# Gated delta rule: the substitution of the 32x32 blocks on GpSimd, with other places for merges, weight loads and splits

## What is computed

```python
proj = h @ w_in                                   # q, k, v, z, beta, a
qkv = silu(causal_depthwise_conv(qkv, conv_w))    # four taps
q, k = l2norm(q) * dh**-0.5, l2norm(k)            # each head used by two value heads
gc = cumsum(g, axis=-1)                           # g from a; per chunk
decay = exp(where(lower, gc[:, None] - gc[None, :], -inf))
a_mat = where(strict, (k * beta) @ k.T * decay, 0)
t_mat = triangular_solve(a_mat + eye, eye)        # inverse of a unit lower triangle
u, w = t_mat @ (v * beta), t_mat @ (k * beta * exp(gc))
qk = where(lower, q @ k.T * decay, 0)
# over the chunks, in order:
v_new = u - w @ state
o = (q * exp(gc)) @ state + qk @ v_new
state = state * exp(g_last) + (k * exp(g_last - gc)).T @ v_new
```

## Time and profile before

| | |
|---|---|
| median of 3 runs | 2576.68 us (2567.54, 2576.68, 2577.74) |
| the profiled execution's own time | 2569.33 us |
| its span, first to last instruction | 2567.5 us |
| granted TensorE clock, mean | 0.924 |
| busy: TensorE / its weight loads | 2159.8 us (84%) / 1669.2 us (65%) |
| busy: VectorE, ScalarE, GpSimd | 1160.5 us (45%), 852.3 us (33%), 500.0 us (19%) |
| L702 to L704, the slices, 784 each | 349.3, 316.8 and 315.8 us |

### The profile page before, as it was taken

The page is one execution under the profiler, slowest core; times in us unless marked ns, Lnnn a source line. Parts: engine busy times, 40 slices in busy tenths (PEclk is TensorE's granted clock), DMA queues, the critical chain, the costliest instruction groups (busy, mean ns, idle before and its releaser), DMA issues. The chain is left out here.

```text
span 2567.5 us, 29131 instructions
## 1 busy us (share of the span) xinstructions
PE 2159.8 (84%) x11176; PEld 1669.2 (65%) x11176; DVE 1160.5 (45%) x2121; ACT 852.3 (33%) x1288; POOL 500.0 (19%) x280
## 2 busy tenths in 40 slices
PE   3588989998898989657798299989989887999978
PEld 2466767776676767545586186667766655788767
DVE  5657566665657474415512432323324231532243
ACT  2354343434343444113301313332333452420031
POOL 0220202010111111004425421111111100532140
PEclk7799999999999999768999699999999898999989
DMA  6122323222222231225312121021120204211222
GB/s 264 48 82 59 103 58 95 53 92 56 88 59 89 57 98 59 52 101 188 110 48 76 52 61 50 25 99 34 50 74 26 74 25 164 90 58 50 74 82 82
DMA packets 126521, 199.21 MB, mean 78 GB/s; under 512 B 56324, under 2 KB 87812, under 8 KB 125232
## 3 DMA queue, kind: packets, MB, share of 16 engines
q1 hardware_dynamic: 126384, 197.34, 24.0%
HBM read 155.17 MB, written 42.11 MB: 77 GB/s over the span
## 5 line engine op out<-in xcount | busy, mean ns | idle before, releaser
L702 PE MATMUL p_job<-h_hi,w_hi 128*128 128x512 f32 x784 | 349.3, 446 | 87.3 <-DVE w_lo L847 83.0
L703 PE MATMUL p_job<-h_lo,w_hi 128*128 128x512 f32 x784 | 316.8, 404 | 0.0
L704 PE MATMUL p_job<-h_hi,w_lo 128*128 128x512 f32 x784 | 315.8, 403 | 0.0
L1688 PE MATMUL m_job<-h_hi,m_hi 128*128 128x512 f32 x592 | 262.0, 443 | 36.7 <-POOL m_lo L1524 36.7
L702 PEld LDWEIGHTS p_job<-h_hi,w_hi 128*128 128x128 f32 x784 | 153.9, 196 | 135.9 <-DVE w_lo L847 94.5
L1690 PE MATMUL m_job<-h_hi,m_lo 128*128 128x512 f32 x592 | 238.7, 403 | 0.0
L1689 PE MATMUL m_job<-h_lo,m_hi 128*128 128x512 f32 x592 | 238.0, 402 | 0.0
L1524 POOL TENSOR_TENSOR m_lo<-m_raw,m_hi 128x1024 fp32r<-128x1024 f32 x37 | 89.9, 2429 | 467.0 <-DVE m_hi L1796 467.0
L703 PEld LDWEIGHTS p_job<-h_lo,w_hi 128*128 128x128 f32 x784 | 154.2, 197 | 34.8 <-issue 7.7
L704 PEld LDWEIGHTS p_job<-h_hi,w_lo 128*128 128x128 f32 x784 | 153.7, 196 | 34.3
L1688 PEld LDWEIGHTS m_job<-h_hi,m_hi 128*128 128x128 f32 x592 | 115.3, 195 | 83.0 <-POOL m_lo L1524 37.4
(11 more groups left out here) (341 smaller groups left out, 4513.7 us busy)
## 6 DMA issues: line engine op xcount, KB each, us to landing
w_raw<-in_w SPq DMA_DIRECT2D x49, 512.0 KB, 3.9
m_raw<-in_w SPq DMA_DIRECT2D x37, 512.0 KB, 3.6
rows<-grows SPq DMA_DIRECT2D x32, 512.0 KB, 6.7
ada<-in_ada_w SPq DMA_DIRECT2D x8, 1536.0 KB, 12.6
e_raw<-in_w SPq DMA_DIRECT2D x24, 512.0 KB, 3.5
z_scr<-pre SPq DMA_DIRECT2D x16, 512.0 KB
o_scr<-oT SPq DMA_DIRECT2D x64, 128.0 KB, 1.8
ob<-o_scr SPq DMA_DIRECT2D x16, 512.0 KB, 4.5
```

Of the source, the lines that this page charges most:

```text
L702: nc.tensor.matmul(p_job[h][:], hi, h_hi[:, k, cut], start=(k == 0), stop=False)
L703: nc.tensor.matmul(p_job[h][:], hi, h_lo[:, k, cut], start=False, stop=False)
L704: last = nc.tensor.matmul(p_job[h][:], lo, h_hi[:, k, cut], start=False, stop=(k == KD - 1))
L1688: nc.tensor.matmul(p_job[h][:], hi, h_hi[:, k, cut], start=(k == 0), stop=False)
```

## The change

The lane steps move from VectorE to GpSimd, in the same form: 62 instructions and the turned copy in each of eight groups. Four numbers in `plan` move: `AHEAD` from 12 to 10, five slices and not four behind each lane step (so `lanes_out` stands behind slice 50 and not 44), and the merges behind slice 78 and not 72. The split stands ahead of a job's slice 1 and not of slice 6. The load ahead of slice 2 is of the job after the next, not of the next. In the lines below L972, L975 and L979 of before are L535, L538 and L542 of the change, and what stands between L523 and L960 is 19 lines further down (L845 is L864, L894 is L913, L910 is L929).

```diff
--- before.py
+++ after.py
@@ -210,7 +210,7 @@
 
 JOBS = 6
 SLOTS = NT + 2
-AHEAD = 12
+AHEAD = 10
 
 
 def plan(i):
@@ -244,10 +244,10 @@
         nonlocal sent, behind
         for _ in range(min(n, len(slices) - sent)):
             s = slices[sent]
-            if s[2:] == (0, 2):
+            if s[2:] == (0, 1):
+                out.append(("split", s[1]))
+            elif s[2:] == (0, 2):
                 out.append(("weights", s[1]))
-            elif s[2:] == (0, 6):
-                out.append(("split", s[1]))
             out.append(s)
             sent += 1
             behind = [(n - 1, x) for n, x in behind]
@@ -282,11 +282,11 @@
     send(AHEAD - sent)
     for q in range(LANE_STEPS):
         out.append(("lane", q))
-        send(4)
+        send(5)
         if ahead and q == 2:
             out.append(("bcast", i))
     out.extend([("lanes_out",), ("diag_in",)])
-    send(72 - sent)
+    send(78 - sent)
     if ahead:
         out.append(("decay", i, 0))
     for q in range(4):
@@ -447,8 +447,8 @@
                 for i in range(N_IT):
                     g = i - 1
                     for s in plans[i]:
-                        if s[0] == "weights" and 2 < job(i, s[1]) + 1 < N_JOBS:
-                            load(job(i, s[1]) + 1)
+                        if s[0] == "weights" and 2 < job(i, s[1]) + 2 < N_JOBS:
+                            load(job(i, s[1]) + 2)
                         elif s[0] == "bcast":
 
                             if i == 0:
@@ -522,7 +522,26 @@
                 for i in range(N_IT):
                     g = i - 1
                     for s in plans[i]:
-                        if s[0] == "decay":
+                        if s[0] == "lane":
+                            q = s[1]
+                            if q == 0:
+                                pool.wait_ge(al_in, 16 * (g + 1))
+                                pool.wait_ge(eye_in, 16 * (g + 1))
+                            for j in range(4 * q, min(4 * q + 4, BLK - 1)):
+                                m, r, w = N_LANE * g + 2 * j, j + 1, BLK - 1 - j
+                                step = lane_tmp[0:LANES, 0:r * w].rearrange("p (c i) -> p c i", i=w)
+                                if m >= 1:
+                                    pool.wait_ge(lane_done, m)
+                                nc.gpsimd.tensor_tensor(step, bc(UL[0:LANES, 0:r, j], 2, w),
+                                                        bc(AL[0:LANES, j, r:], 1, r), ALU.mult).then_inc(lane_done, 1)
+                                pool.wait_ge(lane_done, m + 1)
+                                nc.gpsimd.tensor_tensor(UL[0:LANES, 0:r, r:], UL[0:LANES, 0:r, r:], step,
+                                                        ALU.subtract).then_inc(lane_done, 1)
+                            if q == LANE_STEPS - 1:
+                                pool.wait_ge(lane_done, N_LANE * (g + 1))
+                                nc.gpsimd.tensor_copy(TL[0:LANES], UL[0:LANES].rearrange("p c t -> p t c")
+                                                      ).then_inc(turned, 1)
+                        elif s[0] == "decay":
                             b = s[2]
                             pool.wait_ge(diff_done, 4 * i + b + 1)
                             x = gams(i, b).rearrange("p a b c -> p (a b) c")
@@ -959,25 +978,6 @@
                                 kd[:, 2 * b:2 * b + 2],
                                 bc(p_mone[:, 0:256].rearrange("p (t c) -> p t c", t=2), 2, 2),
                                 bc(edl[:, 2 * b:2 * b + 2, :], 3, P), ALU.mult).then_inc(kd_done, 1)
-                        elif s[0] == "lane":
-                            q = s[1]
-                            if q == 0:
-                                dve.wait_ge(al_in, 16 * (g + 1))
-                                dve.wait_ge(eye_in, 16 * (g + 1))
-                            for j in range(4 * q, min(4 * q + 4, BLK - 1)):
-                                m, r, w = N_LANE * g + 2 * j, j + 1, BLK - 1 - j
-                                step = lane_tmp[0:LANES, 0:r * w].rearrange("p (c i) -> p c i", i=w)
-                                if m >= 1:
-                                    dve.wait_ge(lane_done, m)
-                                nc.vector.tensor_tensor(step, bc(UL[0:LANES, 0:r, j], 2, w),
-                                                        bc(AL[0:LANES, j, r:], 1, r), ALU.mult).then_inc(lane_done, 1)
-                                dve.wait_ge(lane_done, m + 1)
-                                nc.vector.tensor_tensor(UL[0:LANES, 0:r, r:], UL[0:LANES, 0:r, r:], step,
-                                                        ALU.subtract).then_inc(lane_done, 1)
-                            if q == LANE_STEPS - 1:
-                                dve.wait_ge(lane_done, N_LANE * (g + 1))
-                                nc.vector.tensor_copy(TL[0:LANES], UL[0:LANES].rearrange("p c t -> p t c")
-                                                      ).then_inc(turned, 1)
                         elif s[0] == "merge":
                             q = s[1]
                             dve.wait_ge(merge_ready, 4 * g + q + 1)
```

## The result

The changed kernel takes 2664.95 us (median of 4 runs, 2662.78 to 2668.28), the kernel before in the same runs 2577.21 us: a ratio of 1.0349, 95% interval 1.032 to 1.0378, so 3.5% or 87.7 us slower. The forecast was 2670.

What follows compares the result with a forecast made beforehand. The second stage was taken as bound by TensorE, stalled by late weight splits. Seven groups at 6.5 + 4.7 - 0.5 + 1.5 = 12.2 us (85), plus 15 for the last, on 2569.3 gave 2670 us; range 2615 to 2735.

Steps and rivals of the forecast that it cites:

- term 6: TensorE's clock: two slow stretches go, one idle stretch of 13 us comes; +1.5 us a group (0 to 4).
- step 1: Earlier loads and splits remove TensorE's weight stalls: slice 78 is reached 6.8 us earlier than the merge before.
- 2, chain with nothing beside it (last group): Lanes and turned copy on GpSimd, without VectorE's interference: 42.2 us (bounds 29 and 44).
- step 3: VectorE's taps, splits and norm multiplies hold up GpSimd's lanes through SBUF: 12.6 us a group (bounds 0 and 20).
- step 4: Last job's weight load, behind the substitution's seven loads on SyncE, delays the second merge: +4.7 us a group (0 to 7).
- Step 5: Recurrence: three chunks lose their slices; -0.5 us a group (0 to -1.2).
- Step 7: Last group: the turned copy ends later on GpSimd, all of it on the path; +15.4 us (3 to 25).
- the 40 to 44 that were named as a sign: Sign of being right: last group's chain, AL's landing to end of turned copy, takes 40 to 44 us.
- Rival A: Lane instructions slip between VectorE's without blocking, but the last load stays late: 2571 us; chance 0.08.
- Rival B: Short instructions cost GpSimd less and hardly block, a chain of 34 us: faster, 2525 us; chance 0.12.
- Rival C: Short rows or blocking cost GpSimd's lanes 15 us more in each of eight groups: 2790 us; chance 0.06.
- Slice 72 at 475.3: Without stalls and slow matmuls, TensorE would come to the first merge at 475.3 us instead of 486.21.

Runs made afterwards that it cites:

- short_taps: The change with VectorE's three taps of each convolution cut from 1024 columns to 8, leaving work out: 2576.34 us, ratio 1.0008.
- load_before_stores: The change with the weights load at slice 0 instead of 2, so the last job's load precedes the substitution's two stores: 2653.26 us, ratio 1.0319.
- norm_sums_later: early_weights_only with the two key norm sums and their multiplies placed 4 to 8 slices later, and one added VectorE wait: 2586.85 us, ratio 1.0045.
- norm_behind_copies: early_weights_only with the second query norm behind its half job's copy, key norms after it, and an added VectorE wait: 2582.69 us, ratio 1.0037.
- norm_copies_70: norm_behind_copies with the merges behind 70 slices instead of 72 and an added SyncE wait between stores of z: 2587.99 us, ratio 1.0063.
- norm_later_merge_68: norm_sums_later with the merges behind 68 slices instead of 72 and an added SyncE wait between stores of z: 2604.97 us, ratio 1.0121.
- hi_on_scalar: early_weights_only with the rounding of weights to their high part on ScalarE from the fourth job on: 2558.16 us, ratio 0.9947.
- early_weights_only: The kernel before with only the earlier weight loads and splits; lanes on VectorE, merges at slice 72: 2551.86 us, ratio 0.9928.

## Why the prediction was right

The forecast of slower and its size, 2670 against 2665, came out mostly by its own mechanism; the clock of term 6 had another cause than the one named, and the closeness of the two numbers is in part luck. The rows for a group are those of i = 3:

| step | predicted, us | measured, us |
|---|---|---|
| 1, slice 78 done, after the first slice | 58.1 | 56.8 |
| 2, chain with nothing beside it (last group) | 42.2 | 39.7 |
| 3, added by VectorE | 12.6 | 13.3 |
| chain in the group | 54.8 | 53.0 |
| merge later | +6.5 | +4.3 |
| 4, second merge after the first | +4.7 | +4.2 |
| 5, recurrence | -0.5 | 0 |
| 6, clock, second merge to read | +1.5 | +2.7 |
| a group | 12.2 | 11.2 (11.4 in the mean of six, 12.1 up to the read of i = 1) |
| 7, last group | +15.4 | +12.0, and 7.8 in its chunks |
| later stages | 0 | -3.2 |

*Steps 1 to 3.* From the end of slice 78 to the first merge TensorE is idle for 12.40 us, where 10 to 15 were named. The merge is 2.2 us less late than forecast: AL landed 7.6 us after the first slice and not 8.1, and the chain was 1.8 shorter. With nothing beside them the 31-element instructions took 0.24 to 0.26 us and those of 252 to 256 elements 0.63 to 0.72 rather than 0.73, the multiplies less than the subtractions; the turned copy took 1.90 and not 1.5. The last group's chain, 39.7 us, is just below the 40 to 44 that were named as a sign. short_taps bears out what step 3 gives to the nine taps, 7.9 us: without them the chain was 6.8 to 8.6 us shorter in groups i = 2 to 7, 7.6 in the mean. The edits to group i = 0, put at nothing, moved the first slice of i = 1 from 160.68 to 162.17 us.

The lane instruction beside a tap took 1.5 us, and three taps in a row 4.88 where they take 3.92 alone. GpSimd got through about three lane instructions in that time; three taps and three of these at 0.65 to 0.68 us each would be 5.9 us end to end. The Trainium skill's rule (SBUF — State Buffer, "SBUF: two separate sides"), by which the lock holds for a whole instruction and the loser blocks fully, would have made step 3 20 us, by the prediction's estimate; 13.3 was measured. The block itself the trace confirms, and where GpSimd's instruction is long it is nearly whole. In the same group VectorE's cast, 0.69 us alone, took 4.77 beside the product for the queries:

```profile
447.80 4.60 POOL L567 TENSOR_TENSOR qd<-qd,qv 128x2048 f32<-128x2048 f32 x1 [5.41 <-ACT qd L676]
```

```profile
448.18 4.77 DVE L864 CAST w_hi<-w_raw 128x1024 fp32r<-128x1024 f32 x1
```

No wait of TensorE came of it, but the subtract behind it now fell beside the first lane instruction, which took 1.22 us in place of 0.24. The prediction did not look at this pair, which the earlier split brings together.

*Step 4* was right in mechanism and within half a microsecond. load_before_stores shows it as the load's place in the queue, and that getting rid of it lengthens step 3.

*Step 5 failed*: the recurrence took 35.5 us both times. Before, the steps from read to read already went 5.32, 4.93, 5.31, 4.94, 5.32, 4.93, with slices in all but the last; so the 5.32 and 4.93 of the earlier trace rows were odd and even chunks, and not chunks with slices and without. In the change three chunks lost their slices. Two steps fell from 5.3 to 5.04, but two rose from 4.93 to 5.20, the last among them, which held no slices either way.

*Step 6* was undersized by 1.2 us, and its cause was misplaced. It named the idle time ahead of the first merge. In the full groups of the fourteen traces the stretch from the second merge to the first read took 11.8 to 12.4 us wherever TensorE waited at most 1.5 us ahead of the second merge, and 13.6 to 15.1 us wherever it waited 3.2 us or more. The idle time ahead of the first merge makes no such difference: the low figures hold after 15.8 to 18.5 us of it in load_before_stores and after 18.28 in the change's own group i = 1; the high ones hold in norm_sums_later, norm_behind_copies, norm_copies_70 and norm_later_merge_68, which have none. So the 2.7 us go with the wait of step 4, and moving the load takes both away. The idle time ahead of the first merge shows in the work up to the second, at a clock of 0.59 in load_before_stores and 0.69 in the change. In the change this cost nothing of its own, since TensorE waits there for the copy in any case.

*Step 7* has two parts in the measurement. The merge was 12.0 us later relative to the group's first slice, where 15.4 stood; the prediction costed nothing for the recurrence behind it, which took 49.2 us in place of 41.4. Other kernels have 49.2 us after 18.6 and 19.4 us of idle and 42.6 after 33.5, so this 7.8 us may be scatter of the clock in the last group and not the change's doing; one trace of each kernel can't settle it.

*The sum.* What the prediction priced adds up to 100.8 us; the same parts measured, up to the last group's merge, are 12.1 + 68.5 + 12.0 = 92.6. In the profiled pair the 7.8 us of the last chunks make up most of the difference, and the later stages give 3.2 back; their code is the same, and over the fourteen traces they took 1434 to 1446 us. Without the 7.8 us this execution would have taken about 2659. The forecast also started from 2569.3 us, one execution; from the median before, 2577.2, the same sum would have said 2678. Between the medians the change is 87.7 us, 13 less than forecast. So 2665 lies as close to 2670 as it does partly because the base was low.

*Rival A* (no blocking) is refuted by the 1.5 us rows and by short_taps. *Rival B* is refuted: the chain was 53.0 us. *Rival C* as well: 39.7 us alone.

One belief behind step 1 was wrong without harming the sum. "Slice 72 at 475.3" counted stalls and slow matmuls as time that would come back. In the change it does, because VectorE has no lanes ahead of the norm. Wherever they stay on VectorE, waits behind its norm multiply take the place of the stalls, and at most 0.7% of the time is won.

## What to carry to other kernels

An in-order queue that delays one consumer mostly delays several: before costing a stall at its length, look for the next thing in the same queue that another engine waits for, and how late it is. When a dependent chain is moved to an idle engine, count what that engine shares with the old one (here every tap, cast and multiply of VectorE stretched it, 13 us on 40), and count the loads and copies issued behind its result. Moving an issue in such a list shifts the queue behind it: of six edits meant to win more than the early weights alone, none did. Five lost clearly more at the next wait than they won, and hi_on_scalar's ratio lies within the interval of early_weights_only.

## What the runs showed of the hardware

GpSimd's short elementwise instructions took 0.25 us for 31 elements and 0.63 to 0.68 for 252, with 0.08 us between dependent ones, against VectorE's 0.18 to 0.20 and, for 175, 0.33 (GpSimd 0.52). The turned copy took 1.90 us there and 1.03 to 1.08 on VectorE. In the last group, from the first lane instruction to the end of the copy, the chain is 39.6 us on GpSimd and 23.9 on VectorE, 1.7 times. By an estimate from the change's rows it would still have fitted: 7.6 us to the landing, 39.7 for the chain and 8.6 for the transfers are 55.9, and slice 78 is done at 56.8. Blocking took it past that.

The granted clock of the last group's chunks stood at either level for long stretches with no cause that these runs show. After 33.5 us of idle the change took 7.25 us a chunk nearly throughout and short_taps changed to 4.89 after three chunks. The windows of short_taps:

```profile
1089.10:1110.80 21.70, 16.09 (x55) 12.15 (x55) 4.33 (x13) 2.90 (x7) 0.00 (x0) 0.50 0.04 13
1110.80:1125.40 14.60, 9.00 (x54) 6.65 (x54) 3.65 (x12) 2.30 (x6) 0.00 (x0) 1.00 0.09 28
```

The same stretch of the change:

```profile
1182.60:1229.30 46.70, 34.42 (x124) 26.39 (x123) 7.82 (x26) 5.38 (x14) 0.00 (x0) 0.54 0.06 17
```

A chunk takes 7.25 us at a clock of 0.50, which is 1.2 GHz, and 4.89 at 1.00, which is 2.4. What decides between them there stays open.
